# One piece of 512 moving columns for the feed-forward and query products, in place of two pieces of 256

## The chip, the cores and the metric

The kernel runs on one core of one Trainium2 chip. The metric is the device time of one execution in microseconds (us), taken as the median of several runs.

## The reference

Two transformer blocks follow one another on 256 tokens of width 1024, all in float32. The parts that matter here:

```python
# first block, after its two attentions
u = rms_norm(h, pre_ffn_gain)
gate_up = u @ w_ffn_in                                   # 1024 x 5632
f = (silu(gate_up[:, :2816]) * gate_up[:, 2816:]) @ w_ffn_out
h = h + rms_norm(f, post_ffn_gain)
# second block: delta-rule mixer and sparse attention on rmsnorm(x, g_mix), then
hx = rmsnorm(x, g_xattn)
qx = hx @ w_xq                                           # 1024 x 1024, cross-attention queries
...                                                      # attention over mem, w_xo, residual
hf = rmsnorm(x, g_ffn)
x = x + (silu(hf @ w_gate) * (hf @ w_up)) @ w_down       # 1024 x 2816 twice, 2816 x 1024
return rmsnorm(x, g_final)
```

## The kernel before, in words

**Two halves of each number.** TensorE is used with the rounded 32-bit type `F32R`. To keep precision every operand is split in a high part (the rounded value) and a low part (the rest), and a product is made of three matmuls: weight high by activation high, weight high by activation low, weight low by activation high.

**Weights.** They arrive in units of 1 MB (128 partitions x 2048 numbers) in four buffers `raw`, which SyncE fills as they come free. ScalarE writes the high part into `whi`, VectorE the low part into `wlo` (line 1312), in two halves per unit. There are two units of `whi` and `wlo`.

**Activations.** The normed and transposed activations of a block lie in `R1b`, a tile of 128 partitions x 2 x 8 x 272: index 1 is high or low, index 2 the block `kt` of 128 channels, and the last 256 or 272 tokens (272 with the 16 meta tokens of the first block). High and low part of the same `kt` are thus 8 x 272 numbers apart, and two blocks of the same part are 272 numbers apart. `R1[0]` is the high part, `R1[1]` the low part, `R1[2]` both. The tiles `R2`, `R3a`, `R3b` have a high and a low part of 8 x 256 each.

**Who reads `R1b`.** The first block's projections and gates (272 or 256 columns), the second block's mixer projections, and, of concern here: the gate and up products of both feed-forwards (`upg`, `upu`, through `fed`), and the cross-attention queries (`xq`). `turnx` fills `R1b` for these: ScalarE writes the high part (its line 1948), VectorE the low part (line 1302).

**Feed-forward.** It runs over `j` = 0 to 10, blocks of 256 hidden channels. For each `j` come one unit of gate weights, one of up weights (each in two halves of 128 output channels), and one unit of `w_down` for the block `j-1`. For `j` in `WIDE` (1 to 9) a half is done by `wide`: for each of 8 `kt`, one matmul of 512 moving columns (weight high by activation high and low side by side, line 786) and one of 256 (weight low by activation high, line 787). The two halves of the output bank are added later by VectorE. For `j` = 0 (`featk`, lines 775 to 777) and `j` = 10 (`feat`, lines 762 to 764), and in `xq`, three matmuls of 256 columns take their place. `down` (lines 1040 to 1042) has the activation as weights, and moves 512 contiguous columns of `whi` or `wlo`.

The line that reads both parts is

```python
e.matmul(B[:, :].rearrange("p (a n) -> p a n", a=2), hi[:, kt, c], R[2][:, :, kt, 0:256], start=kt == 0, stop=False)
```

The order of the work is a plan written out by `schedule()`, the same for all engines; each engine goes through its part of it in order, with semaphores between them.

Of the kernel before, what the change touches and what calls it, by code (L numbers as in the profile page):

```python
# [12 lines left out]
MUL, ADD, SUB, MAX = ALU.mult, ALU.add, ALU.subtract, ALU.max  # L13
# [436 lines left out]
def program(nc, A, out):  # L450
    with ExitStack() as ctx:
# [3 lines left out]
        def alias(name, n, others):  # L455
            with nc.sbuf_tensor(name, [128, n], F32) as t:
                pass
            return t, [sb(o, s, F32R) for o, s in others]
# [2 lines left out]
        whi = [sb(f"whi{i}", [128, UN], F32R) for i in range(HL)]  # L461
        wlo = [sb(f"wlo{i}", [128, UN], F32R) for i in range(HL)]
        SR1, (R1b,) = alias("SR1", 8 * NT * 2, [("R1b", [128, 2, 8, NT])])
        R1 = (R1b[:, 0], R1b[:, 1], R1b)
        SC, R2 = alias("SC", 4096, [("R2h", [128, 8, 256]), ("R2l", [128, 8, 256])])
        SD, R3b = alias("SD", 4096, [("R3bh", [128, 8, 256]), ("R3bl", [128, 8, 256])])
        SA, R3a = alias("SA", 4096, [("R3ah", [128, 8, 256]), ("R3al", [128, 8, 256])])
# [13 lines left out]
        def signal(name, by=1):  # L481
            signals.append(Signal(ctx.enter_context(nc.semaphore(name)), now, by))
            return signals[-1]
# [8 lines left out]
        gemm = signal("gemm")  # L492
        set_dve, set_act = signal("set_dve"), signal("set_act")
        norm_pe, norm_act, norm_dve, norm_pool = [signal("norm_" + n) for n in ("pe", "act", "dve", "pool")]
# [7 lines left out]
        ffn_act, ffn_dve = signal("ffn_act"), signal("ffn_dve")  # L502
# [5 lines left out]
        query_act = signal("query_act")  # L508
# [8 lines left out]
        def ps(*key):  # L517
            return held[key]
# [4 lines left out]
        def stat(key, n):  # L523
            if key not in stats:
                stats[key] = st[:, room[0]:room[0] + n]
                room[0] += n
                assert room[0] <= 512
            return stats[key]

        ident = ca[:, 0:128]  # L530
        half = stat("half", 16)
# [7 lines left out]
        def f32(ap):  # L539
            return ap.bitcast(F32)  # L540
# [14 lines left out]
        def unit(i):  # L555
            _, k, n = unit_src(i)
            return [t[i % HL][:, 0:k * n].rearrange("p (k n) -> p k n", k=k) for t in (whi, wlo)]
# [57 lines left out]
        def par_of(name):  # L615
            return lambda b: par(name, b)

        NORM = {
            "n1": (X, xs0, R1, par_of("pre_mix"), "small"), "nm": (memt, xsm, R3b, par_of("g_mem"), "all"),
            "nx2": (X, xs2, R1, par_of("g_mix"), "all")}  # L620
        APART = ("nx2",)
# [3 lines left out]
        GAIN = {"nf1": par_of("pre_ffn"), "nxa": par_of("g_xattn"), "nf2": par_of("g_ffn")}  # L625
# [20 lines left out]
        def normed(s):  # L646
            return lambda kt, t=1: (norm_dve, (s, "lo", kt))
# [86 lines left out]
        def tensor(e, counting):  # L734
            p = Lane(e, counting)

            def claim(pool, key, *freed):

                b = next_bank(pools[pool])
                for signal_, k in b.freed:  # L740
                    p.wait_ge(signal_, k)
                b.freed = freed
                held[key] = b.t
                return b.t
# [10 lines left out]
            def feat(o, i, j, R, n, ready, *keys):  # L755

                hi, lo = unit(i)
                c = slice(j * 128, j * 128 + 128)
                p.wait_ge(lo_split, (i, j))
                for kt in range(8):  # L760
                    p.wait_ge(*ready(kt))
                    e.matmul(o, hi[:, kt, c], R[0][:, kt, 0:n], start=kt == 0, stop=False)  # L762
                    e.matmul(o, hi[:, kt, c], R[1][:, kt, 0:n], start=False, stop=False)  # L763
                    m = e.matmul(o, lo[:, kt, c], R[0][:, kt, 0:n], start=False, stop=kt == 7)  # L764
                m.then_inc(gemm(("half", i, j), ("unit", i), *keys))

            def featk(B, i, part, R, ready, key):

                hi, lo = unit(i)
                p.wait_ge(lo_split, (i, part))  # L770
                for kt in range(4 * part, 4 * part + 4):
                    p.wait_ge(*ready(kt))
                    for j in range(2):
                        o, c = B[:, 256 * j:256 * j + 256], slice(j * 128, j * 128 + 128)
                        e.matmul(o, hi[:, kt, c], R[0][:, kt, 0:256], start=(kt, j) == (0, 0), stop=False)
                        e.matmul(o, hi[:, kt, c], R[1][:, kt, 0:256], start=False, stop=False)
                        m = e.matmul(o, lo[:, kt, c], R[0][:, kt, 0:256], start=False, stop=(kt, j) == (7, 1))
                m.then_inc(gemm(("half", i, part), ("unit", i), key))

            def wide(B, i, j, R, ready):  # L780

                hi, lo = unit(i)
                c = slice(j * 128, j * 128 + 128)
                for kt in range(8):
                    p.wait_ge(*ready(kt))
                    e.matmul(B[:, :].rearrange("p (a n) -> p a n", a=2), hi[:, kt, c], R[2][:, :, kt, 0:256], start=kt == 0, stop=False)  # L786
                    m = e.matmul(B[:, 0:256], lo[:, kt, c], R[0][:, kt, 0:256], start=False, stop=kt == 7)  # L787
                return m

            def fed(kind, f, j, part, i):  # L790
                ready = normed("nf1" if f == "f1" else "nf2")
                if j not in WIDE:
                    return pair(kind, (f, j), part, i, "four", R1, ready, (ffn_dve, (kind, f, j)))
                B = claim("four", (kind, f, j, part), (ffn_dve, (kind, f, j, part)))
                p.wait_ge(lo_split, (i, part))
                wide(B, i, part, R1, ready).then_inc(gemm(("half", i, part), ("unit", i), (kind, f, j, part)))

            def tok(i, part, R, n, ready, *targets, opens=0, half_done=True):

# [68 lines left out]
            def rope(key, b, j, i, k):  # L868
                n = ROPE[key][1]
                B = claim("gemm", ("rope", k), (rope_act, k), (rope_dve, ("cos", k)))  # L870
                if n > NR:
                    p.wait_ge(norm_dve, ("n1", "lo", 8))
                feat(B[:, 0:n], i, j, R1, n, normed("n1"), ("rope", k))

            def ropek(part, i):
# [6 lines left out]
                for kt in range(4 * part, 4 * part + 4):  # L882
                    p.wait_ge(norm_dve, ("n1", "lo", kt))
                    for k in range(2):
                        o, c = ps("rope", k)[:, 0:256], slice(k * 128, k * 128 + 128)
                        e.matmul(o, hi[:, kt, c], R1[0][:, kt, 0:256], start=kt == 0, stop=False)
                        e.matmul(o, hi[:, kt, c], R1[1][:, kt, 0:256], start=False, stop=False)
# [100 lines left out]
            def pair(kind, u, j, i, pool, R, ready, *freed):  # L988
                if j == 0:
                    claim(pool, (kind, u), *freed)  # L990
                if order[i][1] == "featk":
                    return featk(ps(kind, u), i, j, R, ready, (kind, u))
                feat(ps(kind, u)[:, 256 * j:256 * j + 256], i, j, R, 256, ready, (kind, u))
# [24 lines left out]
            def upg(f, j, part, i):  # L1018
                fed("g", f, j, part, i)

            def upu(f, j, part, i):
                fed("u", f, j, part, i)
# [234 lines left out]
                        mm(B[r0:r0 + 64, 0:256], wuv[:, i, :], OL[:, i % 4, :]).then_inc(dsa_pe(("dm", h // 2), ("wuv", i)))  # L1257

            def xq(u, j, i):
                pair("xq", u, j, i, "big", R1, normed("nxa"), (query_act, u))  # L1260

            def cross(h, part):
                if part == "s":
# [16 lines left out]
                if part == "o":  # L1280
                    B = claim("four", ("xo", h), (cross_dve, ("ox", h)))
                    p.wait_ge(cross_dve, ("pt", h))
                    for j in range(2):
# [5 lines left out]
            parts = {"turn": turn, "turnx": turnx, "rsb": rsb_, "rope": rope, "ropek": ropek, "turnm": turnm, "v": v, "vt": vt, "swa": swa, "diff": diff, "gate": gate, "bsw": bsw, "bdf": bdf,  # L1289
                     "out": out_, "mem": mem, "upg": upg, "upu": upu, "down": down, "tail": tail, "conv": conv, "zg": zg,  # L1290
                     "delta": delta, "dsa": dsa, "dsah": dsah, "xq": xq, "cross": cross}
            p.wait_ge(set_dve, "half")
            keep(banks[7].t, 13, half[:, 0:1].to_broadcast([128, 128]), half[:, 0:1].to_broadcast([128, 256]))
# [4 lines left out]
        def vector(e, counting):  # L1298
            d = Lane(e, counting)

            def stt(o, a, s, b, op0, op1):
                return e.scalar_tensor_tensor(out=o, in0=a, scalar=s, in1=b, op0=op0, op1=op1)
# [29 lines left out]
            def turnx(s, u):  # L1332
                d.wait_ge(norm_act, (s, "hi", 2 * u + 1))
                for b in (2 * u, 2 * u + 1):
                    stt(R1[1][:, b, 0:256], ps(s, "T", 2 * u)[:, b % 2 * 256:b % 2 * 256 + 256], GAIN[s](b),
                        f32(R1[0][:, b, 0:256]), MUL, SUB).then_inc(norm_dve((s, "lo", b)))

            def stat_(s):

# [604 lines left out]
        def scalar(e, counting):  # L1944
            a = Lane(e, counting)

            def act(o, i, f=ACT.Copy, **kw):
                return e.activation(o, i, f, **kw)  # L1948
# [19 lines left out]
            def turnx(s, u):  # L1968
                a.wait_ge(norm_pe, (s, "T", 2 * u))
                for b in (2 * u, 2 * u + 1):  # L1970
                    act(R1[0][:, b, 0:256], ps(s, "T", 2 * u)[:, b % 2 * 256:b % 2 * 256 + 256], scale=GAIN[s](b)).then_inc(
                        norm_act((s, "hi", b)))

            def stat_(s):
# [616 lines left out]
```

## Time and profile before

| what | value |
|---|---|
| device time, median of 3 runs | 996.69 us (995.23 to 997.12) |
| profiled execution, first to last instruction (span) | 994.9 us |
| TensorE matmul busy | 972.3 us, 98% |
| VectorE busy | 691.0 us, 69% |
| ScalarE busy | 539.5 us, 54% |
| GpSimd busy | 131.2 us, 13% |
| granted TensorE clock, mean | 0.996 |

For the profiled execution the span is the only time on record; the medians come from runs of their own, and include what lies before the first and after the last instruction. Busy times of matmuls are unions in time: a matmul is shown from its start to its modelled end, and the next one starts before that, so the rate of TensorE is read from the starts.

### The profile page before, as it was taken

The page shows a single profiled execution, that of the slowest core. Times are in us where ns is not written, and L with a number is a line of the kernel's source. Part 1 is how long each engine was busy: PE and PEld are TensorE (multiplying, and loading weights), DVE is VectorE, ACT ScalarE, POOL GpSimd, SP SyncE. Part 2 cuts the span into 40 slices and gives each one's busy share as a digit, 9 for nine tenths or more (in the row PEclk, how much of TensorE's full clock was granted, in tenths as well). Part 3 has the DMA queues.
Part 4 walks back from the last instruction along what each step waited for, and adds up shares of the span by engine and source line. Part 5 has one row for each costly group of instructions (what it writes and reads, how often), then busy time and mean ns, then how long its engine had stood idle before and what let it go on. Part 6 is the DMA issues. An engine that isn't in the chain of part 4 may idle for free.

```text
span 994.9 us, 16733 instructions
## 1 busy us (share of the span) xinstructions
PE 972.3 (98%) x6780; PEld 882.4 (89%) x6780; DVE 691.0 (69%) x1280; ACT 539.5 (54%) x1039; POOL 131.2 (13%) x145
## 2 busy tenths in 40 slices
PE   8999999999999999999999999899899999999997
PEld 8999898898999988888989988898799998888886
DVE  6887776776478676767576778966665477767675
ACT  7776767664456644444445885544444364444443
POOL 2211112211042000000010149501100000000001
PEclk9999999999999999999999999999999999999999
DMA  9533333333358555555557642201352365555541
GB/s 320 181 128 129 127 128 127 128 127 123 136 171 262 180 193 189 189 191 187 195 188 230 212 128 85 85 1 43 128 169 86 107 212 171 195 185 195 185 169 43
DMA packets 126108, 154.99 MB, mean 156 GB/s; under 512 B 2728, under 2 KB 117680, under 8 KB 125648
## 3 DMA queue, kind: packets, MB, share of 16 engines
q1 hardware_dynamic: 123616, 142.91, 43.2%
q0 software_dynamic: 1952, 10.61, 3.0%
q8 instruction: 54, 0.88, 0.4%
q10 hardware_dynamic: 464, 0.40, 0.1%
q14 instruction: 22, 0.18, 0.1%
HBM read 150.76 MB, written 3.16 MB: 155 GB/s over the span
## 4 chain that ended last, share of the span: by engine, by line
PE 80%; DVE 9%; ACT 6%; POOL 2%; issue 2%; DMA 1%; POOLq 0%; DVEq 0%; ACTq 0%
PE ps L786 13%; PE ps L762 8%; PE ps L787 7%; PE ps L764 7%; PE ps L763 7%; PE ps L1067 5%; PE ps L1040 4%; PE ps L1041 4%; PE ps L1042 4%; PE ps L806 3%; PE ps L808 3%; PE ps L807 3%; PE ps L748 3%; DVE wlo L1312 3%; ACT whi L1948 2%; PE ps L907 2%
## 5 line engine op out<-in xcount | busy, mean ns | idle before, releaser
L1312 DVE TENSOR_TENSOR wlo<-raw,whi 128x1024 fp32r<-128x1024 f32 x268 | 326.5, 1235 | 172.4 <-ACT whi L1948 171.8
L1948 ACT ACTIVATE whi<-raw 128x1024 fp32r<-128x1024 f32 x268 | 274.5, 1051 | 144.2 <-PE ps L787 53.6
L786 PE MATMUL ps<-R1b,whi 128*128 128x512 f32 x576 | 201.8, 393 | 0.0
L762 PE MATMUL ps<-R1b,whi 128*128 128x256 f32 (+1 forms) x592 | 173.1, 292 | 0.8 <-DVE wlo L1312 0.8
L764 PE MATMUL ps<-R1b,wlo 128*128 128x256 f32 (+1 forms) x592 | 167.7, 283 | 0.0
L763 PE MATMUL ps<-R1b,whi 128*128 128x256 f32 (+1 forms) x592 | 167.5, 283 | 0.0
L787 PE MATMUL ps<-R1b,wlo 128*128 128x256 f32 x576 | 161.4, 280 | 0.0
L786 PEld LDWEIGHTS ps<-R1b,whi 128*128 128x128 f32 x576 | 108.1, 188 | 24.7 <-issue 0.5
L762 PEld LDWEIGHTS ps<-R1b,whi 128*128 128x128 f32 x592 | 111.5, 188 | 11.4 <-issue 9.2
L763 PEld LDWEIGHTS ps<-R1b,whi 128*128 128x128 f32 x592 | 111.5, 188 | 0.4 <-issue 0.2
L764 PEld LDWEIGHTS ps<-R1b,wlo 128*128 128x128 f32 x592 | 111.8, 189 | 0.0
L787 PEld LDWEIGHTS ps<-R1b,wlo 128*128 128x128 f32 x576 | 108.2, 188 | 0.6
L2343 POOL TENSOR_TENSOR st<-st 128x1 f32<-128x1 f32 (+5 forms) x28 | 24.0, 865 | 387.3 <-DVE st L1305 307.3
L1040 PE MATMUL ps<-whi,R3ah 128*128 128x512 f32 x176 | 69.0, 392 | 1.1 <-DVE wlo L1312 1.1
L1041 PE MATMUL ps<-wlo,R3ah 128*128 128x512 f32 x176 | 68.8, 391 | 0.0
L1042 PE MATMUL ps<-whi,R3al 128*128 128x512 f32 x176 | 68.5, 389 | 0.0
L1948 ACT ACTIVATE F<-F 128x512 f32<-128x512 f32 (+6 forms) x58 | 29.2, 506 | 56.6 <-DVE F L1565 53.7
L1948 ACT ACTIVATE R3ah<-F 128x512 fp32r<-128x512 f32 x22 | 13.9, 632 | 68.1 <-DVE F L1587 68.1
L1554 DVE TENSOR_REDUCE F<-ps 128x256 f32<-128x512 f32 x72 | 49.1, 683 | 0.0
L1948 ACT ACTIVATE SC<-ps 32x256 f32<-32x256 f32 (+3 forms) x76 | 32.1, 424 | 19.7 <-PE ps L764 8.9
L1040 PEld LDWEIGHTS ps<-whi,R3ah 128*128 128x128 f32 x176 | 33.0, 188 | 9.1 <-issue 1.9
L1042 PEld LDWEIGHTS ps<-whi,R3al 128*128 128x128 f32 x176 | 33.0, 188 | 7.2
(299 smaller groups left out, 2023.9 us busy)
## 6 DMA issues: line engine op xcount, KB each, us to landing
raw<-in_w_in SPq DMA_DIRECT2D x35, 1024.0 KB, 5.1
raw<-in_w_ffn_in SPq DMA_DIRECT2D x22, 1024.0 KB, 5.1
raw<-in_w_ffn_out SPq DMA_DIRECT2D x11, 1024.0 KB, 5.4
raw<-in_w_gate SPq DMA_DIRECT2D x11, 1024.0 KB, 5.3
raw<-in_w_up SPq DMA_DIRECT2D x11, 1024.0 KB, 5.4
raw<-in_w_down SPq DMA_DIRECT2D x11, 1024.0 KB, 5.8
raw<-in_w_out SPq DMA_DIRECT2D x8, 1024.0 KB, 5.4
raw<-in_w_xkv SPq DMA_DIRECT2D x8, 1024.0 KB, 5.5
```

The lines of the kernel that those rows point to most:

```text
L762: e.matmul(o, hi[:, kt, c], R[0][:, kt, 0:n], start=kt == 0, stop=False)
L763: e.matmul(o, hi[:, kt, c], R[1][:, kt, 0:n], start=False, stop=False)
L764: m = e.matmul(o, lo[:, kt, c], R[0][:, kt, 0:n], start=False, stop=kt == 7)
L786: e.matmul(B[:, :].rearrange("p (a n) -> p a n", a=2), hi[:, kt, c], R[2][:, :, kt, 0:256], start=kt == 0, stop=False)
L787: m = e.matmul(B[:, 0:256], lo[:, kt, c], R[0][:, kt, 0:256], start=False, stop=kt == 7)
L1040: e.matmul(B[:, :], Fh[:, k, c], hi[:, k, d], start=j == 0 and k == 0, stop=False)
L1041: e.matmul(B[:, :], Fh[:, k, c], lo[:, k, d], start=False, stop=False)
L1042: m = e.matmul(B[:, :], Fl[:, k, c], hi[:, k, d], start=False, stop=end and k == 1)
L1067: return e.matmul(o, a, b, start=True, stop=True)
L1312: e.tensor_tensor(half_of(wlo[i % HL], i, k), half_of(raw[i % RAW], i, k), f32(half_of(whi[i % HL], i, k)), SUB).then_inc(lo_split(i, (i, k)))
L1554: e.tensor_reduce(FSLOT[j % 2][0][:, at:at + 256], B[:, :].rearrange("p (a n) -> p n a", a=2), AX, ADD).then_inc(ffn_dve((kind, f, j, b)))
L1948: return e.activation(o, i, f, **kw)
```

## The change

The same storage gets a second view for the feed-forwards and the query product, `RX`: 8 blocks of 512 numbers, the high part of a block in the first 256 of them and its low part right behind. High and low part of one `kt` are then contiguous, and blocks lie 512 numbers apart. `wide` reads the 512 columns as one piece; all that writes or reads this data (`turnx` on both engines, `fed`, `xq`) goes through the new view. The first block's projections and the second block's mixer keep the old view `R1`. No instruction is added, removed or moved in the plan.

```diff
-        R1 = (R1b[:, 0], R1b[:, 1], R1b)
+        R1 = (R1b[:, 0], R1b[:, 1])
+        R1c = R1b[:, :, :, :].rearrange("p a k n -> p (a k n)")[:, 0:4096].rearrange("p (k m) -> p k m", k=8)
+        RX = (R1c[:, :, 0:256], R1c[:, :, 256:512], R1c)
...
-                    e.matmul(B[:, :].rearrange("p (a n) -> p a n", a=2), hi[:, kt, c], R[2][:, :, kt, 0:256], start=kt == 0, stop=False)
+                    e.matmul(B[:, :], hi[:, kt, c], R[2][:, kt, :], start=kt == 0, stop=False)
...
-                    return pair(kind, (f, j), part, i, "four", R1, ready, (ffn_dve, (kind, f, j)))
+                    return pair(kind, (f, j), part, i, "four", RX, ready, (ffn_dve, (kind, f, j)))
...
-                wide(B, i, part, R1, ready).then_inc(gemm(("half", i, part), ("unit", i), (kind, f, j, part)))
+                wide(B, i, part, RX, ready).then_inc(gemm(("half", i, part), ("unit", i), (kind, f, j, part)))
...
-                pair("xq", u, j, i, "big", R1, normed("nxa"), (query_act, u))
+                pair("xq", u, j, i, "big", RX, normed("nxa"), (query_act, u))
...
-                    stt(R1[1][:, b, 0:256], ps(s, "T", 2 * u)[:, b % 2 * 256:b % 2 * 256 + 256], GAIN[s](b),
-                        f32(R1[0][:, b, 0:256]), MUL, SUB).then_inc(norm_dve((s, "lo", b)))
+                    stt(RX[1][:, b, :], ps(s, "T", 2 * u)[:, b % 2 * 256:b % 2 * 256 + 256], GAIN[s](b),
+                        f32(RX[0][:, b, :]), MUL, SUB).then_inc(norm_dve((s, "lo", b)))
...
-                    act(R1[0][:, b, 0:256], ps(s, "T", 2 * u)[:, b % 2 * 256:b % 2 * 256 + 256], scale=GAIN[s](b)).then_inc(
+                    act(RX[0][:, b, :], ps(s, "T", 2 * u)[:, b % 2 * 256:b % 2 * 256 + 256], scale=GAIN[s](b)).then_inc(
```

## Rows read from the trace of the kernel before

**Rows 1.** The page: span, busy time by engine, granted clock in 40 slices.

```profile
span 994.9 us, 16733 instructions
PE 972.3 (98%) x6780; PEld 882.4 (89%) x6780; DVE 691.0 (69%) x1280; ACT 539.5 (54%) x1039; POOL 131.2 (13%) x145
PEclk9999999999999999999999999999999999999999
```

**Rows 2.** Busy time in stretches: two inside the feed-forwards.

```profile
core 0: us, PE busy (x) PEld busy (x) DVE busy (x) ACT busy (x) POOL busy (x), PEclk, DMA share, GB/s
...
351.50:484.60 133.10, 133.10 (x705) 114.28 (x704) 92.79 (x105) 57.43 (x66) 0.00 (x0) 1.00 0.56 192
...
814.00:975.00 161.00, 161.00 (x888) 139.82 (x887) 112.04 (x127) 70.35 (x81) 0.00 (x0) 1.00 0.52 177
```

**Rows 3.** Groups of TensorE instructions, shapes apart: busy us, mean ns of one.

```profile
L786 PE MATMUL ps<-R1b,whi 128*128 128x512 f32 x576 | 201.8, 393 | 0.0
L787 PE MATMUL ps<-R1b,wlo 128*128 128x256 f32 x576 | 161.4, 280 | 0.0
...
L1040 PE MATMUL ps<-whi,R3ah 128*128 128x512 f32 x176 | 69.0, 392 | 1.1 <-DVE wlo L1312 1.1
```

**Rows 4.** Timeline of TensorE over one round, a `j` of the first feed-forward: start, length.

```profile
368.31 0.39 PE L786 MATMUL ps<-R1b,whi 128*128 128x512 f32 x1
368.53 0.28 PE L787 MATMUL ps<-R1b,wlo 128*128 128x256 f32 x1
368.65 0.39 PE L786 MATMUL ps<-R1b,whi 128*128 128x512 f32 x1
...
379.34 0.28 PE L787 MATMUL ps<-R1b,wlo 128*128 128x256 f32 x1
379.46 0.40 PE L1040 MATMUL ps<-whi,R3ah 128*128 128x512 f32 x1
379.69 0.40 PE L1041 MATMUL ps<-wlo,R3ah 128*128 128x512 f32 x1
...
382.22 0.39 PE L1040 MATMUL ps<-whi,R3ah 128*128 128x512 f32 x1
...
384.71 0.39 PE L1042 MATMUL ps<-whi,R3al 128*128 128x512 f32 x1
384.94 0.39 PE L786 MATMUL ps<-R1b,whi 128*128 128x512 f32 x1
```

**Rows 5.** Timeline of TensorE: matmuls of 256 columns that move `R1b`, `j` = 10.

```profile
484.74 0.28 PE L762 MATMUL ps<-R1b,whi 128*128 128x256 f32 x1
484.85 0.28 PE L763 MATMUL ps<-R1b,whi 128*128 128x256 f32 x1
484.97 0.28 PE L764 MATMUL ps<-R1b,wlo 128*128 128x256 f32 x1
...
490.30 0.28 PE L764 MATMUL ps<-R1b,wlo 128*128 128x256 f32 x1
490.42 0.28 PE L762 MATMUL ps<-R1b,whi 128*128 128x256 f32 x1
```

**Rows 6.** Timeline of TensorE: matmuls of 256 columns that move `R3b`.

```profile
262.50 0.28 PE L776 MATMUL ps<-R3bl,whi 128*128 128x256 f32 x1
262.62 0.28 PE L777 MATMUL ps<-R3bh,wlo 128*128 128x256 f32 x1
262.74 0.28 PE L775 MATMUL ps<-R3bh,whi 128*128 128x256 f32 x1
...
267.18 0.28 PE L776 MATMUL ps<-R3bl,whi 128*128 128x256 f32 x1
267.30 0.28 PE L777 MATMUL ps<-R3bh,wlo 128*128 128x256 f32 x1
```

**Rows 7.** `R1b` from 300 to 360 us: lengths (ns, min/median/max) of what `turnx` writes.

```profile
L1948 ACT ACTIVATE R1b<-ps,pc x8: 464/474/493, 316.2 to 326.6; 128x256 fp32r<-128x256 f32 x8
L1302 DVE SCALAR_TENSOR_TENSOR R1b<-ps,pc,R1b x8: 474/474/478, 320.7 to 328.0; 128x256 fp32r<-128x256 f32 x8
```

## Prediction

> **What bounds the kernel now.** I read the page first. TensorE is busy in 98% of the span, VectorE in 69%, ScalarE in 54% [rows 1], so the question is what sets TensorE's rate. The granted clock is at the top of its digits in all slices, so the clock is not in play. Then I read the busy times of stretches inside the two feed-forwards, where nearly all of the changed work lies: TensorE is busy for 133.10 us of 133.10 and for 161.00 of 161.00, at a granted clock of 1.00 (its upper level, 2.4 GHz), while VectorE has 92.79 and 112.04 us [rows 2]. The reader is to see that nothing else limits these stretches: a nanosecond won or lost per matmul arrives whole at the end.
>
> The groups of instructions come next. The 576 wide matmuls (line 786) last 393 ns, two pieces of 256 moving columns each. Line 1040 moves 512 contiguous columns of `whi`, and lasts 392 ns [rows 3]. These lengths overlap with the next matmul, so they can't price the change, but they already say that the seam between two pieces is not worth tens of nanoseconds. The price has to be read from the starts.
>
> **The rate from starts.** One round (one `j`) begins at 368.31 and the next at 384.94 us, 16.63 us. Up to 379.46 there are 32 pairs of a wide and a narrow matmul: 11.15 us / 32 = 348.4 ns for a pair. Then 24 matmuls of `down` follow in 5.48 us. Their first 12 (379.46 to 382.22) take 2.76 us / 12 = 230.0 ns, their last 12 (382.22 to 384.94) 2.72 / 12 = 226.7 ns [rows 4]. That is the rate of a contiguous 512-column matmul whose data starts on a multiple of 512 numbers, which is just what the changed wide matmul will read.
>
> For 256 columns there are two kinds of rows. With `R1b`, whose blocks are 272 numbers apart, 48 starts from 484.74 to 490.42 give 5.68 / 48 = 118.3 ns [rows 5]. With `R3b`, whose blocks are 256 numbers apart, 40 starts from 262.50 to 267.30 give 4.80 / 40 = 120.0 ns [rows 6]. So the evenly laid tile is no faster than the oddly laid one; it is slower by 1.7 ns per matmul. What causes it the rows don't say, but the changed layout (blocks 512 numbers apart) belongs with `R3b`, not with the old `R1b`.
>
> **The change part by part.**
>
> *The wide matmul becomes one piece.* There are 9 values of `j`, 2 feed-forwards, 2 products, 2 halves and 8 `kt`: 9 x 2 x 2 x 2 x 8 = 576 [rows 3]. A pair costs 348.4 ns now. Afterwards I take 226.7 + 120.0 = 346.7 ns, the two evenly laid rows. Saved: 1.7 ns x 576 = 1.0 us. The bounds: if the narrow one of the pair keeps the 118.3 ns of the old layout, the pair costs 345.0 and 3.4 x 576 = 2.0 us are saved. If the wide one runs as the first 12 matmuls of `down` do, at 230.0, the pair costs 350.0 and 1.6 x 576 = 0.9 us are lost. I take the middle value because the last 12 starts are the settled ones, and because 120.0 is what a narrow matmul costs on every tile laid like the new one.
>
> *The cost of the seam by itself* can be read as the difference: 348.4 - 118.3 = 230.1 ns for the two-piece matmul, against 226.7 for the contiguous one. At most 3.4 ns, about eight cycles at 2.4 GHz, hang on the seam, and the first 12 of `down` show 230.0 without any seam [rows 4]. So even this may not be the seam's.
>
> A rule of the Trainium skill speaks against the change, beside these rows: "Advanced Engine Details and Errata", section "Memory Cachelines", says that SBUF is read in lines of 16 bytes, and that reading goes at full rate as long as following accesses stay in the same line. Both pieces are runs of 256 adjacent numbers, that is 64 whole lines, so that by the rule one piece crosses as many lines as two, and the first term would be zero. The sum would then be +1.0 us in place of 0.0, by the narrow matmuls below alone. The trace doesn't decide between them: 230.0 and 226.7 stand in one and the same group.
>
> *The narrow matmuls outside of the pairs.* They read the new view too: `j` = 0 and `j` = 10 of both feed-forwards, with 2 x 2 x 2 = 8 units of 48 matmuls, and the queries with 4 units of 48. Together 12 x 48 = 576. By [rows 5, 6] each goes from 118.3 to 120.0: +1.7 x 576 = +1.0 us. The bound below is nothing (the layout has no effect, 0.0). TensorE is as full at `j` = 0 and 10 as elsewhere; in the query stage it now and then waits for others, which would hide part of it. So 1.0 is the upper end.
>
> *What `turnx` writes.* For each of three norms 8 ScalarE and 8 VectorE instructions write 256 adjacent numbers as before, 474 ns each [rows 7]; only the address changes. I cost it at 0. No cover is needed for that: shape, type and source are as before. If writing to the new place cost 5% more (24 ns, a bound from the spread of 464 to 493 in the row), at most one norm's chain of 8 stands on the path: 0.2 us, three times, 0.6 us.
>
> *What is not touched.* No instruction, wait or DMA is moved, so that no queue changes its order. The one-piece matmul writes the same 512 columns of the same bank.
>
> **The sum** for the profiled execution: -1.0 (pairs) + 1.0 (other narrow ones) + 0 (turnx) = 0.0 us, so the span stays at 994.9 us. The median of the runs shown is 1.8 us above that span, which I carry over unchanged: 996.7 us. By a hair I lean to the lower side, since the queries hide a part of their loss, and predict 996.6 us.
>
> **The rivals.**
>
> 1. *Gain of the pair without the loss.* The pair runs at 345.0 ns and the narrow ones keep 118.3: -2.0 us, 994.7 us. For it: the seam's 3.4 ns are real, and the slow 120.0 may belong to something else of `R3b`, say its smaller step of 256. Against it: the cross-over would need the wide one to behave as even data and the narrow one as odd data, out of the same tile. It decides for "faster" only if the saving passes 3.5 ns per pair. Chance 0.10.
>
> 2. *The pair gets worse.* A narrow matmul before a wide one may be what costs extra time, as the matmuls of `down` that follow the pairs need some rounds to settle: 379.46 to 379.69 is 0.23, and the first 12 average 230.0 [rows 4]. If in the new layout each wide one starts its data on the same step as the weight load beside it, and takes 233 where the old one took 230.1 (the same 3.3 ns more that lies between first and last 12), a pair costs 233.3 + 120.0 = 353.3: +4.9 x 576 = +2.8 us, and +1.0 of the narrow ones: 1000.5 us. This is a slower kernel by 0.4%. From +1.8 ns per pair on, with the narrow ones' loss, it is slower by over 0.2%. Against it: a contiguous 512 from `whi` settles at 226.7 whatever loads beside it. Chance 0.07.
>
> 3. *The seam keeps the matmul off the array's rate.* The rows give 226.7 - 120.0 = 106.7 ns for 256 more columns, 213.4 for 512; if only the seam and its address step stood between the wide matmul and that, 16.7 ns x 576 = 9.6 us would be saved: 987.1 us. Against it: the contiguous ones need 226.7 themselves, with 13.3 ns on top of the columns, and so do the narrow ones (120.0 - 106.7 = 13.3). It falls with that, but for an effect no row shows. Chance 0.01.
> "TensorE: Matmul & The Clock Gate", section "Wait — 56ns, not 53.3ns?" of the Trainium skill gives such a rate, the columns at 2.4 GHz and some 2.5 ns more, for 16-bit data; the trace disagrees for this kernel's 32-bit matmuls, 226.7 against 215.7 ns [rows 4].
>
> **How the numbers follow.** 0.2% of this time is 2.0 us, about what a measurement of this kernel can tell from no change. My forecast and its bounds (-2.0 to +1.9 us) lie within that, with a chance of 0.82; the runs of the kernel before spread by 1.9 us themselves. Faster: rivals 1 and 3, 0.11. Slower: rival 2, 0.07. The range reaches from 994.6 (rival 1) to 998.9 (the upper bounds of pair, narrow ones and writes, 0.9 + 1.0 + 0.3).
>
> **What would show it.** In the changed kernel's trace the wide matmuls' starts should leave 227 ns (not 230) before the narrow one, and the narrow ones 120 (not 118), so that a round takes 32 x 346.7 + 5.48 = 16.57 us where it took 16.63. At `j` = 10 the 48 starts should take 5.76 us, not 5.68. The groups' mean lengths should stay at about 393 and 280 ns. The prediction is wrong if the round moves by more than 0.1 us, or if the time moves while the rounds don't: then a stage that I hold to be untouched has changed.

## The result: the changed kernel is slower by 0.38%

The changed kernel takes 1000.36 us (median of 5 runs, 998.42 to 1000.81), the kernel before 996.69 us (995.23 to 997.35). The ratio is 1.0038, with a 95% interval of 1.0027 to 1.0049, that is 2.7 to 4.9 us slower. The forecast was 996.6 us, and its range ended at 998.9. The spans below are those of one profiled execution of each kernel.

The page of the changed kernel's profile, the lines that answer to [rows 1]:

```profile
span 996.6 us, 16733 instructions
PE 974.0 (98%) x6780; PEld 881.8 (88%) x6780; DVE 691.2 (69%) x1280; ACT 540.0 (54%) x1039; POOL 131.5 (13%) x145
PEclk9999999999999999999999999999999999999999
```

The number of instructions is the same, and so is the engine that sets the time. The groups of TensorE instructions, shapes apart (busy us, mean ns of one), answer to [rows 3]; two lines were added to the source, so line 788 is the old 786:

```profile
L788 PE MATMUL ps<-R1b,whi 128*128 128x512 f32 x576 | 204.0, 398 | 0.0
L789 PE MATMUL ps<-R1b,wlo 128*128 128x256 f32 x576 | 161.7, 281 | 0.0
```

The wide matmul is shown 5 ns longer (398 against 393). The timeline of TensorE over one round of the first feed-forward (start, length), the lines that answer to [rows 4]:

```profile
368.65 0.39 PE L788 MATMUL ps<-R1b,whi 128*128 128x512 f32 x1
368.87 0.28 PE L789 MATMUL ps<-R1b,wlo 128*128 128x256 f32 x1
368.99 0.40 PE L788 MATMUL ps<-R1b,whi 128*128 128x512 f32 x1
...
379.94 0.40 PE L1042 MATMUL ps<-whi,R3ah 128*128 128x512 f32 x1
...
382.72 0.39 PE L1042 MATMUL ps<-whi,R3ah 128*128 128x512 f32 x1
...
385.44 0.39 PE L788 MATMUL ps<-R1b,whi 128*128 128x512 f32 x1
```

Here is the loss. 32 pairs take 379.94 - 368.65 = 11.29 us, 352.8 ns each, where they took 348.4. The first 12 matmuls of `down` take 231.7 ns (230.0 before), the last 12 take 226.7 as before. A round is 16.79 us, 0.16 more. The third to the ninth round of both feed-forwards are alike in this, within 0.01 us, in each of the two kernels. The first two are not, and one of them teaches something. It is the second round of the second feed-forward, in the changed kernel:

```profile
832.31 0.39 PE L788 MATMUL ps<-R1b,whi 128*128 128x512 f32 x1
...
835.12 0.42 PE L788 MATMUL ps<-R1b,whi 128*128 128x512 f32 x1
835.37 0.28 PE L789 MATMUL ps<-R1b,wlo 128*128 128x256 f32 x1
...
837.92 0.39 PE L788 MATMUL ps<-R1b,whi 128*128 128x512 f32 x1
...
843.47 0.39 PE L1042 MATMUL ps<-whi,R3ah 128*128 128x512 f32 x1
```

Its 32 pairs take 11.16 us, and the last 16 of them (837.92 to 843.47) 5.55 / 16 = 346.9 ns each, with the same matmuls on the same addresses as in the rounds at 352.8. Up to the ninth pair they keep the rhythm of the other rounds, in which the starts behind a wide matmul come after 232, 241 and 236 ns by turns. In the ninth it is 255 ns (835.12 to 835.37) where 241 would be due, and from there to the end the pairs keep the lower cost. So the layout doesn't fix a single cost: at least two steady rhythms exist with it, and which one a round falls into depends also on how it started.

Over all 18 rounds (9 in each feed-forward) the pairs lose 2.0 us and the `down` matmuls behind them 0.3 us.

At `j` = 10, 48 starts of 256-column matmuls, the lines that answer to [rows 5]:

```profile
486.20 0.28 PE L764 MATMUL ps<-R1b,whi 128*128 128x256 f32 x1
...
491.95 0.28 PE L764 MATMUL ps<-R1b,whi 128*128 128x256 f32 x1
```

5.75 us / 48 = 119.8 ns, against 118.3 before. What `turnx` writes, the lines that answer to [rows 7], is as good as unchanged (476 and 478 ns in place of 474):

```profile
L1950 ACT ACTIVATE R1b<-ps,pc x8: 464/476/492, 316.3 to 326.7; 128x256 fp32r<-128x256 f32 x8
L1304 DVE SCALAR_TENSOR_TENSOR R1b<-ps,pc,R1b x8: 474/478/482, 320.7 to 328.0; 128x256 fp32r<-128x256 f32 x8
```

**The whole account.** From the first matmul that reads the new view to the last `down` group, per feed-forward. First the timeline of the kernel before, then that of the changed kernel:

```profile
322.69 0.28 PE L775 MATMUL ps<-R1b,whi 128*128 128x256 f32 x1
...
496.10 0.39 PE L1040 MATMUL ps<-whi,R3ah 128*128 128x512 f32 x1
...
736.98 0.36 PE L775 MATMUL ps<-R1b,whi 128*128 128x256 f32 x1
...
802.84 0.36 PE L775 MATMUL ps<-R1b,whi 128*128 128x256 f32 x1
...
976.32 0.39 PE L1040 MATMUL ps<-whi,R3ah 128*128 128x512 f32 x1
```

```profile
322.73 0.28 PE L777 MATMUL ps<-R1b,whi 128*128 128x256 f32 x1
...
497.71 0.40 PE L1042 MATMUL ps<-whi,R3ah 128*128 128x512 f32 x1
...
736.95 0.36 PE L777 MATMUL ps<-R1b,whi 128*128 128x256 f32 x1
...
803.09 0.36 PE L777 MATMUL ps<-R1b,whi 128*128 128x256 f32 x1
...
978.00 0.40 PE L1042 MATMUL ps<-whi,R3ah 128*128 128x512 f32 x1
```

The first feed-forward took 173.41 us and now takes 174.98, the second 173.48 and 174.91: +1.57 and +1.43, together +3.0 us. Between them two things meet. From the first matmul of the query product, which reads the new view too (736.98 and 736.95), to the second feed-forward, 65.86 us have become 66.14: +0.3 us. That makes +3.3 us for the change, inside the interval of the ratio. But from the end of the first feed-forward to the queries, in the mixer and the sparse attention, which keep the old view, the changed kernel is faster by 1.64 us (239.24 against 240.88), so that the spans differ by only 1.7 us. The busy time of TensorE in stretches (busy, instructions, granted clock) shows why. In the kernel before:

```profile
640.00:660.00 20.00, 18.14 (x139) 0.91 0.11 37
...
640.00:645.00 5.00, 3.15 (x20) 0.81 0.41 145
645.00:650.00 5.00, 5.00 (x39) 0.85 0.01 3
```

and in the changed one:

```profile
640.00:660.00 20.00, 18.15 (x149) 1.00 0.17 53
...
640.00:645.00 5.00, 3.15 (x23) 1.00 0.65 210
```

The whole difference arises there: a matmul of the changed kernel comes 1.6 us later than its counterpart of before at 640 us, and at the same moment at 660 us. It isn't the change's doing, for an execution of the changed layout that had the low clock too (two_pieces_new_layout, an experiment below) doesn't gain it. Two of its matmuls, and the stretch:

```profile
323.04 0.28 PE L777 MATMUL ps<-R1b,whi 128*128 128x256 f32 x1
...
979.91 0.40 PE L1042 MATMUL ps<-whi,R3ah 128*128 128x512 f32 x1
...
640.00:660.00 20.00, 18.16 (x134) 0.91 0.16 53
```

From its first matmul on the new view to its last `down` group it takes 656.87 us. The kernel before takes 653.63 (976.32 - 322.69), 3.2 us less, at the same clock of 0.91. TensorE is busy for only 3.15 us of the 5 from 640 to 645, before and after, yet the clock fell in one execution and not in the other; what decides it isn't shown. Two single profiles can thus differ by half of this effect for a reason of another stage. A stretch that runs at the full clock in both, as the feed-forwards do, can be compared to a few hundredths of a microsecond. The runs without a trace show it as well: those of the kernel before fall into groups near 995.0, 996.7 and 998.4 us.

### The profile page after: what moved, and what is told of

It reads as the page before. It is cut to its first block, busy times and chain, and to the rows that moved or that the text cites. A ratio compares the mean times of both kernels' runs of the same rounds, so it can differ in the third digit from the quotient of the medians.

```text
span 996.6 us, 16733 instructions
## 1 busy us (share of the span) xinstructions
PE 974.0 (98%) x6780; PEld 881.8 (88%) x6780; DVE 691.2 (69%) x1280; ACT 540.0 (54%) x1039; POOL 131.5 (13%) x145
## 4 chain that ended last, share of the span: by engine, by line
PE 80%; DVE 9%; ACT 6%; POOL 2%; issue 2%; DMA 1%; POOLq 0%; DVEq 0%; ACTq 0%
PE ps L788 14%; PE ps L764 8%; PE ps L789 7%; PE ps L766 7%; PE ps L765 7%; PE ps L1069 5%; PE ps L1042 4%; PE ps L1044 4%; PE ps L1043 4%; PE ps L808 3%; PE ps L810 3%; PE ps L809 3%; PE ps L750 3%; DVE wlo L1314 3%; ACT whi L1950 2%; PE ps L909 2%
## 5 line engine op out<-in xcount | busy, mean ns | idle before, releaser
L788 PE MATMUL ps<-R1b,whi 128*128 128x512 f32 x576 | 204.0, 398 | 0.0
```

What stands on the lines that cost most here:

```text
L788: e.matmul(B[:, :], hi[:, kt, c], R[2][:, kt, :], start=kt == 0, stop=False)
```

## The experiments

All runs are read in the same way as above, in the third round of the first feed-forward: the start of its first wide matmul, of the first `down` matmul behind it, 32 pairs in between. The rounds from the third to the ninth agree in every run, in both feed-forwards. A step of 0.01 us in a start is 0.3 ns of a pair. "Distance" is the number of bytes by which the blocks of moving data lie off a multiple of 256 bytes, relative to the weights. It is worked out from the sizes and the order of the tiles in the program; the traces hold no addresses. The blocks of weights themselves start 512 bytes or a multiple of it apart. Each ratio is to the kernel before as it ran in the same series.

| run | distance | us for 32 pairs | ns per pair | ratio to before (95%) |
|---|---|---|---|---|
| kernel before | 0, 64, 128, 192 by turns | 11.15 | 348.4 | 1 |
| changed kernel | 0 | 11.29 | 352.8 | 1.0038 (1.0027 to 1.0049) |
| two_pieces_new_layout | 0 | 11.29 | 352.8 | 1.0047 (1.0031 to 1.0063) |
| step_528 | 0, 64, 128, 192 by turns | 11.15 | 348.4 | 1.0004 (0.9992 to 1.0016) |
| order_new_layout | 0 | 11.14 | 348.1 | 1.0010 (1.0000 to 1.0020) |
| order_old_layout | as before | 11.18 | 349.4 | 1.0005 (0.9996 to 1.0015) |
| shift_8 | 32 | 11.11 | 347.2 | 0.9985 (0.9976 to 0.9994) |
| shift_8_again | 32 | 11.11 | 347.2 | 0.9986 (0.9976 to 0.9995) |
| shift_16 | 64 | 11.17 | 349.1 | 1.0001 (0.9991 to 1.0010) |
| shift_24 | 96 | 11.21 | 350.3 | 1.0026 (1.0014 to 1.0037) |
| shift_32 | 128 | 11.22 | 350.6 | 1.0013 (1.0003 to 1.0024) |
| shift_64 | 256 | 11.29 | 352.8 | 1.0026 (1.0016 to 1.0036) |
| step_544 | 0, 128 by turns | 11.14 | 348.1 | 1.0004 (0.9993 to 1.0014) |
| narrow_to_other_half | 0 | 11.29 | 352.8 | 1.0039 (1.0026 to 1.0052) |
| gap_before_weights | 0 (both moved by 32) | 11.29 | 352.8 | 1.0047 (1.0030 to 1.0063) |
| weights_moved_only | 96 | 11.21 | 350.3 | 1.0037 (1.0023 to 1.0051) |
| gap_behind_weights | 32, all tiles | 11.11 | 347.2 | 1.0000 (0.9989 to 1.0010) |
| gap_behind_weights_old | old layout + 32, all tiles | 11.20 | 350.0 | 1.0014 (1.0005 to 1.0024) |

The theory after the result: the seam has nothing to do with it; what costs time is where the moving data starts, now that all blocks start at the same place within some unit. Its rivals: reading 512 columns as one piece is slower in itself, or it is the alternation of wide and narrow matmuls.

### One piece or two, and the step between blocks

```diff
-                    e.matmul(B[:, :], hi[:, kt, c], R[2][:, kt, :], start=kt == 0, stop=False)
+                    e.matmul(B[:, :].rearrange("p (a n) -> p a n", a=2), hi[:, kt, c], R[2][:, kt, :].rearrange("p (a n) -> p a n", a=2), start=kt == 0, stop=False)
```

> The changed kernel, whose wide matmul reads the same adjacent 512 columns, but as two pieces of 256. Theory A (where the data lies costs the time, not the number of pieces): pairs stay at 352.8 ns, time as the changed kernel, 1000.4 us. Theory B (reading 512 columns as one piece is itself slower): pairs go back to 348.4 to 349.2 ns, time 998.0 to 998.4 us. Theory C (alternation of a wide and a narrow matmul costs, whatever is read): as A.

Measured: 352.8 ns, 1000.36 us beside 995.42 of the kernel before on the same chip. Reading in one piece or in two makes no difference, as theory A said.

```diff
-        R1c = R1b[:, :, :, :].rearrange("p a k n -> p (a k n)")[:, 0:4096].rearrange("p (k m) -> p k m", k=8)
-        RX = (R1c[:, :, 0:256], R1c[:, :, 256:512], R1c)
+        R1c = R1b[:, :, :, :].rearrange("p a k n -> p (a k n)")[:, 0:4224].rearrange("p (k m) -> p k m", k=8)
+        RX = (R1c[:, :, 0:256], R1c[:, :, 256:512], R1c[:, :, 0:512])
```

> The changed kernel with its blocks 528 numbers apart (2112 bytes) in place of 512, one piece of 512 columns. Theory A: the uneven step brings back what the old layout had, pairs 346 to 349 ns, and the 256-column matmuls outside of pairs 118.3 ns in place of 120.0; time 996 to 998 us. Theory B: pairs stay at 352.8 ns, and only the narrow ones gain, 1.0 us: 999.4 us. Theory C: as B.

Measured: 348.4 ns, 996.65 beside 995.42 us. The timeline of TensorE over one round of this kernel:

```profile
368.30 0.39 PE L788 MATMUL ps<-R1b,whi 128*128 128x512 f32 x1
...
379.45 0.40 PE L1042 MATMUL ps<-whi,R3ah 128*128 128x512 f32 x1
...
384.93 0.39 PE L788 MATMUL ps<-R1b,whi 128*128 128x512 f32 x1
```

16.63 us for the round, the 16.63 of the kernel before [rows 4], with one piece of 512 columns and an odd step. So the whole loss of the pairs comes from where the blocks start, here by the step of 512 numbers, and adjacency brings nothing: with the same starts modulo 256 bytes, one piece and two cost the same.

### The order within the pairs

```diff
                 for kt in range(8):
                     p.wait_ge(*ready(kt))
-                    e.matmul(B[:, :], hi[:, kt, c], R[2][:, kt, :], start=kt == 0, stop=False)
-                    m = e.matmul(B[:, 0:256], lo[:, kt, c], R[0][:, kt, 0:256], start=False, stop=kt == 7)
+                    for narrow in (kt % 2 == 1, kt % 2 == 0):
+                        if narrow:
+                            m = e.matmul(B[:, 0:256], lo[:, kt, c], R[0][:, kt, 0:256], start=False, stop=False)
+                        else:
+                            m = e.matmul(B[:, :], hi[:, kt, c], R[2][:, kt, :], start=kt == 0, stop=kt == 7)
```

> The changed kernel with the matmuls of two blocks turned: wide, narrow, narrow, wide, so that half of the changes between wide and narrow are gone. Theory C (the change from narrow to wide costs some 6 ns): two pairs cost 699 to 700 ns in place of 705.6, time 998.6 us. Theory A (addresses alone): no change, 1000.4 us, or any other value, since each wide matmul then runs beside the load of another block's weights. Theory B: no change, 1000.4 us.

> The kernel before with the same turned order: wide, narrow, narrow, wide, two pieces, old layout. Theory C: two pairs cost 694 to 696 ns in place of 697 to 698, time 995.5 to 996 us. Theories A and B: no change beyond 0.1%, 996.7 us.

Measured: 348.1 ns on the new layout (696 for two pairs, less than any theory said), 349.4 on the old one (699 for two, more than before). Theory C, by which the alternation as such costs time, would have the same sign twice, and falls. But the order matters: it gains 4.7 ns where the starts all fall together and loses 1.0 where they don't. The distance doesn't explain that, since it is 0 for every block in either order. Together with the round at 346.9 ns above this says that the distance is one cause of two: how wide and narrow matmuls and weight loads follow one another in time is the other. Why the turned order helps isn't shown.

### Moving the view

The first line of the view becomes `[:, 16:4112]` for shift_16, and so on; one number is 4 bytes. For step_544 it is `[:, 0:4352]`, with `RX[2]` cut to 512 columns.

```diff
-        R1c = R1b[:, :, :, :].rearrange("p a k n -> p (a k n)")[:, 0:4096].rearrange("p (k m) -> p k m", k=8)
+        R1c = R1b[:, :, :, :].rearrange("p a k n -> p (a k n)")[:, 8:4104].rearrange("p (k m) -> p k m", k=8)
```

> The changed kernel, step 512, with the whole view moved by 16 numbers (64 bytes), so that every block starts 64 bytes off where it starts now. Theory A1 (the place of a start within 128 bytes sets the cost, and the place 64 bytes off is the cheap one): pairs about 345 ns, time 995.4 to 996 us. Theory A2 (the change of place from block to block is what helps): pairs stay at 352.8 ns, time 1000.4 us.

> The changed kernel with the view moved by 8 numbers (32 bytes). Theory A1 with 64 bytes as the unit that counts: a value that 64-byte steps do not show, between 345 and 353 ns or above. Theory A2: 352.8 ns, 1000.4 us.

> The changed kernel with blocks 544 numbers (2176 bytes) apart: they start on a multiple of 128 bytes, but by turns on a multiple of 256 or 128 off it. Theory A1 with 128 bytes as the unit: pairs stay at 352.8 ns, 1000.4 us. If the unit is 256 bytes or more: pairs 348 to 350 ns, 997 to 998 us.

Measured: 349.1, 347.2 and 348.1 ns; 996.12, 994.97 and 996.17 us beside 996.69. A2 (only a change of place helps) falls: in shift_16 and shift_8 all blocks start at the same place, and yet pairs are 3.7 and 5.6 ns faster than in the changed kernel. A1 stands, but not as expected: 64 bytes is not the cheap place (345 was expected), 32 is better, and 128 bytes is not the unit. The round of shift_8 on the timeline of TensorE:

```profile
368.55 0.40 PE L788 MATMUL ps<-R1b,whi 128*128 128x512 f32 x1
...
379.66 0.39 PE L1042 MATMUL ps<-whi,R3ah 128*128 128x512 f32 x1
...
385.12 0.40 PE L788 MATMUL ps<-R1b,whi 128*128 128x512 f32 x1
```

### The output's place

```diff
-                    m = e.matmul(B[:, 0:256], lo[:, kt, c], R[0][:, kt, 0:256], start=False, stop=kt == 7)
+                    m = e.matmul(B[:, 256:512], lo[:, kt, c], R[0][:, kt, 0:256], start=False, stop=kt == 7)
```

> The changed kernel with the narrow matmul of a pair adding to columns 256 to 511 of its bank in place of 0 to 255; the two halves are added up later anyway. Theory A (the reads from the activations' tile): pairs stay at 352.8 ns, 1000.4 us. A rival, by which the output's place in the bank makes the wait: pairs change by 2 ns or more, time by 1.2 us or more.

Measured: 352.8 ns, 999.70 us beside 996.69. Where the narrow matmul writes in its bank is not the cause.

### Relative to what: moving the weights

gap_before_weights puts an unused tile of 8 numbers ahead of `whi`, so that weights and activations move together; weights_moved_only adds to that a view that starts at 24; gap_behind_weights and gap_behind_weights_old put the tile between weights and activations, in the changed kernel and in the kernel before.

```diff
+        sb("gap", [128, 8])
         whi = [sb(f"whi{i}", [128, UN], F32R) for i in range(HL)]
         wlo = [sb(f"wlo{i}", [128, UN], F32R) for i in range(HL)]
```

> The changed kernel with an unused tile of 8 numbers (32 bytes) allocated ahead of the split weights, so that weights, activations and all tiles behind them move by 32 bytes together. Theory R (what counts is the place of the moving data relative to the weights loaded beside it): pairs stay at 352.8 ns, 1000.4 us. Theory P (the place of the moving data by itself counts): as with shift_8, pairs 347.3 ns, 995 us.

> The same unused tile ahead of the weights, and the view of the activations moved on by 24 numbers, so that its blocks start on multiples of 128 bytes as in the changed kernel, while the weights start 32 bytes off. Theory R: pairs about 347 ns, 995 to 996 us. Theory P: pairs stay at 352.8 ns, 1000.4 us.

Measured: 352.8 ns (999.90 us beside 995.30) and 350.3 ns (998.76 us). The activations of gap_before_weights lie 32 bytes further on, as in shift_8, and there is nothing of the gain of shift_8. So the place by itself doesn't count (theory P falls); it is the distance to the weights. In weights_moved_only the activations lie 128 bytes on and the weights 32, so their distance is 96 bytes. The 347 ns expected were wrong, since I had taken a distance of 96 to be as good as 32; shift_24 below tests that.

```diff
         wlo = [sb(f"wlo{i}", [128, UN], F32R) for i in range(HL)]
+        sb("gap", [128, 8])
         SR1, (R1b,) = alias("SR1", 8 * NT * 2, [("R1b", [128, 2, 8, NT])])
```

> The changed kernel with the unused tile of 8 numbers between the weights and the activations: every tile of activations moves by 32 bytes against the weights. Pairs 347.3 ns as with shift_8 by both theories; beyond that the 256-column matmuls on the other tiles may go from 120.0 to 118 ns (some 1,100 of them: 2 us) by either, and the down products, whose moving data are the weights, only by theory R. Time 992.5 to 995 us.

> The kernel before with the same unused tile between weights and activations, old layout, two pieces. Both theories: pairs 347 to 348 ns in place of 348.6, other tiles as in gap_behind_weights. Time 993 to 996 us; if it equals gap_behind_weights, the layout of the change is worth nothing even at its best place.

Measured: 347.2 ns for the pairs of the first, but 994.95 us beside 995.30, a ratio of 1.0000 (0.9989 to 1.0010), which shows no gain. The timeline of TensorE over a round of gap_behind_weights shows where it goes:

```profile
367.03 0.40 PE L789 MATMUL ps<-R1b,whi 128*128 128x512 f32 x1
...
378.14 0.40 PE L1043 MATMUL ps<-whi,R3ah 128*128 128x512 f32 x1
...
383.51 0.40 PE L1045 MATMUL ps<-whi,R3al 128*128 128x512 f32 x1
383.74 0.40 PE L789 MATMUL ps<-R1b,whi 128*128 128x512 f32 x1
```

The 24 matmuls of `down` now take 5.60 us, 233.3 ns each, where they took 5.48 in the kernel before and 5.46 in shift_8. In `down` the roles are turned round: `whi` moves, `R3a` is loaded. The same 32 bytes, seen from the other side, are 256 - 32 = 224, and cost it 0.12 us in each round, more than the 0.04 that the pairs win against the kernel before. That `down` would change at all is what only the theory of the distance had said; which way, it had left open. The other part of the expectation came in part: the 256-column matmuls on the other tiles gain, and the first wide matmul of the first feed-forward starts at 333.51 us (334.86 before). In the old layout the gap makes the pairs slower (350.0 where 347 to 348 was expected) and `down` too: 1.0014.

### The period, and the best version again

> The changed kernel with the view moved by 32 numbers (128 bytes). If the pattern repeats every 128 bytes: pairs 352.8 ns, 1000 us. If it repeats every 256 bytes or more: pairs below 352 ns, as the step of 544 numbers hints (348.1).

> The changed kernel with the view moved by 64 numbers (256 bytes). If the pattern repeats every 256 bytes: pairs 352.8 ns, 1000 us. If over more: another value.

> The changed kernel with the view moved by 24 numbers (96 bytes). In weights_moved_only the weights were 32 bytes on and the activations 0, that is 96 bytes back within 128; if only the distance counts and it repeats every 128 bytes, pairs are 350.2 ns here too, time 998 to 999 us.

> The same kernel as shift_8 (the view of the changed kernel moved by 8 numbers), timed again in more rounds. If the place of the data is the cause, the pairs are 347.3 ns again and the time is 0.1 to 0.2% below the kernel before; if the first result was chance in the clock of another stage, the ratio comes back to 1.000.

Measured: 350.6, 352.8 and 350.3 ns (998.14, 998.77 and 998.90 us beside 996.75), and 347.2 ns again for shift_8_again, 995.34 us. At 256 bytes the value of 0 is back, at 128 it isn't: the pattern repeats after 256 bytes as far as these two points show. The distance of 96 bytes gives 350.3 both when the view is moved and when weights and view are, as expected, which is a second sign that the distance counts. The round of shift_64 in the timeline of TensorE, beside the one of the changed kernel above (11.29 both):

```profile
368.73 0.39 PE L788 MATMUL ps<-R1b,whi 128*128 128x512 f32 x1
...
380.02 0.40 PE L1042 MATMUL ps<-whi,R3ah 128*128 128x512 f32 x1
```

And shift_8 is faster than the kernel before: 0.9985 and 0.9986 in two series on two chips, with intervals that end at 0.9994 and 0.9995. It is the version to keep: the change's layout, begun 8 numbers further on. The last 16 pairs of its rounds take 346.7 ns each, which is what the prediction had expected of the change (347.2 is the mean of all 32).

## Why the prediction was wrong, point by point

**What bounds the kernel**: right. TensorE's starts set the time; a few nanoseconds in 576 pairs and in the narrow matmuls of `j` = 0 and 10 arrived whole, +3.0 us over the two feed-forwards. One reading in this part was wrong: that the clock isn't in play. A digit of 9 on the page stands for a slice's mean of 0.90 or more, and the 10 us at 0.81 and 0.85 disappear in such a mean. That stretch doesn't touch the feed-forwards, but it is worth 1.6 us between executions.

**The wide matmul becomes one piece**: this step failed. "Afterwards I take 226.7 + 120.0 = 346.7 ns, the two evenly laid rows"; it is 352.8. So the first term of the sum, -1.0 us, came out as +2.0. The 226.7 came from `down`, where the tile that moves and the tile that is loaded are others, and it was carried to a pair as if a matmul's cost were its own. It isn't: with the same instruction and the same pieces it changes with the distance between the moving data and the weights loaded beside it (347.2 to 352.8 ns for a pair), and with the rhythm that the round has fallen into (352.8 or 346.9 at distance 0). The upper bound, 350.0, was also too low, since it was a mean over the first 12 of the same `down`: both values offered came from another pair of tiles. The 0.3 us that `down` itself loses behind slower pairs had no term in the sum.

**The seam**: the doubt was right, and stronger than it was put. "At most 3.4 ns hang on the seam": it is 0, by two_pieces_new_layout (352.8 against 352.8) and step_528 (348.4 against 348.4). The rule of "Memory Cachelines" in the Trainium skill's "Advanced Engine Details and Errata", by which, as the prediction works it out, a seam at a whole line is free, agrees with that; the +1.0 us that followed from it was too low, as it leaves the distance out.

**The narrow matmuls**: right in sign and size. At `j` = 10 they take 119.8 ns against the 120.0 that was taken, 1.5 ns more for each, and the queries lose 0.3 us.

**What `turnx` writes, and what is not touched**: right. The writes last 476 and 478 ns, and the account above leaves no room for more. The difference in the mixer, 1.64 us, goes with the granted clock of 0.91 of one execution. The range is not quite what its parts say (0.3 us for the writes, where their own bound was 0.6, and 994.6 where rival 1 gives 994.7), but that is too little to matter.

**The rivals**: the second one came true, in number (353.3 ns per pair against 352.8) and in the mechanism that its condition names, "starts its data on the same step as the weight load beside it". Its sum, 1000.5 us, is close to the measured 1000.36, but partly by luck: it has +3.8 us where the traces account for 3.3, and its 233.3 + 120.0 is split otherwise in the trace, where the wide matmuls of the round leave 235.6 ns to the next start and the narrow ones 117.3. It had a chance of 0.07, and the argument against it ("a contiguous 512 from `whi` settles at 226.7 whatever loads beside it") was false; gap_behind_weights shows 233.3 for the same matmuls. The range ended at 998.9 because that rival was left out of it. Rivals 1 and 3 are excluded: no round of the changed kernel settled at 345.0 or less.

**What would show it**: the test named was a round that moves by more than 0.1 us. It moved by 0.16.

What stays open: which part of the memory or of TensorE makes two reads disturb each other, and why one rhythm sets in and not another. The distance isn't the whole of it. Five of these kernels have their pairs at distance 0 or 256 (the changed one, two_pieces_new_layout, narrow_to_other_half, gap_before_weights and shift_64). Of their ten second rounds six end at 346.7 ns a pair (their last 16 pairs) and four at 353 to 354, while all of their later rounds are at the higher value. The value isn't a sum over blocks, either: step_544, whose distances are 0 and 128 by turns, takes 348.1 ns and not the mean of 352.8 and 350.6. For the pairs a distance of 192 bytes was tried only by turns with others and 224 not on its own, nor were steps smaller than 32.

## What to carry to other kernels

Where TensorE is full and each matmul of 256 or 512 columns brings its own weights, the place of the moving tile against the weights' tile was worth 1.6% of a pair's time and 3% of a `down` matmul's. Blocks that all start at the same place modulo 256 bytes as the weights were the worst case for the pairs, and a shift of 32 bytes the best of those tried; for `down`, where the tiles change roles, the same shift was the worse one. It is found by trying a few shifts and reading the starts over some 30 pairs, where 0.3 ns can be seen, since the time of the whole kernel spreads by more. A cost read from one matmul must not be carried to another whose loaded tile lies elsewhere.

## What the runs showed that was not expected

A matmul's cost isn't independent of the weights that are loaded beside it. With nothing changed but the distance between the two tiles, a pair takes 347.2 to 352.8 ns, and a `down` matmul 226.7 or 233.3. And with nothing changed at all, the pairs of one kernel run at 352.8 ns in most rounds and at 346.9 in the last half of one. The Trainium skill, "TensorE: Matmul & The Clock Gate", section "Step-by-step: what each phase is for", says that TensorE has two independent read ports, and that loading the next weights doesn't steal bandwidth from the running matmul. Whether bandwidth is what is lost, no run shows; but for this kernel's 32-bit data the two are not independent, by 1.6% (5.6 ns of 352.8). Also, one profiled execution had a granted clock of 0.91 between 640 and 660 us where another had 1.00, with 1.6 us between them in stages that the change doesn't touch.
